# Hymba step, last stage: the gather of a chunk's second-choice rows is issued one chunk behind the first-choice gather instead of three

## What is computed

```python
def _layer(...):
    mix, ... = _mixer(x, ...)
    x = _layer_norm(DEEPNORM_ALPHA * x + mix, ln1_g, ln1_b)
    x = _layer_norm(DEEPNORM_ALPHA * x + _hmoe(x, ...), ln2_g, ln2_b)

def _hmoe(x, ...):
    # two experts per token: wts (n, 2), eid (n, 2)
    gate = jnp.einsum('nk,nke->ne', wts, jax.nn.one_hot(eid, N_EXPERTS))
    a = jnp.einsum('nd,edf->nef', xt, w1)
    u = jnp.einsum('nd,edf->nef', xt, w3)
    hdn = jax.nn.silu(a) * u * gate[..., None]
    return jnp.einsum('nef,efd->nd', hdn, w2)
```

## Time and profile before

| | us |
|---|---|
| median of 3 executions | 1198.36 |
| lowest, highest | 1190.17, 1199.01 |
| the profiled execution | 1197.36 |
| its span in the trace | 1195.4 |

### The profile page before, as it was taken

One profiled execution on the slowest core, in us unless ns is written; L12 is line 12 of the kernel. 1 busy time (PEld: TensorE's weight loads), 2 busy tenths in 40 slices (PEclk: granted clock), 3 DMA queues, 4 the chain that ended last, 5 costly groups with the idle time before them and its releaser, 6 DMA issues.

```text
span 1195.4 us, 17214 instructions
## 1 busy us (share of the span) xinstructions
PE 1009.2 (84%) x6738; PEld 606.5 (51%) x6738; DVE 600.9 (50%) x1007; ACT 248.9 (21%) x532; POOL 244.1 (20%) x208
## 2 busy tenths in 40 slices
PE   7999999979999695999999999842788999799500
PEld 4666666645656354566666666442344455345200
DVE  1550133347777767787787778353122333231046
ACT  1542111121211122132223222110111111011023
POOL 0000000001110132353454344000000000450175
PEclk9999999989999898999999999955799999899755
DMA  9010101020000244000100110507799787948496
GB/s 385 35 70 1 71 1 71 0 74 1 1 1 1 80 163 178 4 33 19 36 36 1 36 36 18 194 27 289 317 327 351 283 322 299 381 177 305 141 219 181
DMA packets 30680, 154.28 MB, mean 129 GB/s; under 512 B 5546, under 2 KB 5994, under 8 KB 21274
## 3 DMA queue, kind: packets, MB, share of 16 engines
q1 hardware_dynamic: 24938, 130.17, 28.9%
q0 software_dynamic: 5248, 18.94, 6.0%
q10 hardware_dynamic: 432, 4.35, 1.0%
HBM read 321.52 MB, written 23.82 MB: 289 GB/s over the span
## 4 chain that ended last, share of the span: by engine, by line
PE 78%; DMA 9%; DVE 7%; issue 3%; POOL 1%; ACT 1%; SPq 1%; DVEq 0%; ACTq 0%; POOLq 0%
PE psum L1657 17%; PE psum L772 9%; PE psum L1708 9%; PE psum L759 9%; PE psum L1334 5%; PE psum L1311 5%; PE psum L1345 5%; PE psum L800 4%; DMA weight_slots<-in_w_gate 3%; DMA x_cm<-y_slots,hg_k 2%; DMA hg_decay<-in_w_up 2%; PE psum L734 1%; PE psum L1675 1%; PE psum L1296 1%; POOL x_cm L1425 1%
## 5 line engine op out<-in xcount | busy, mean ns | idle before, releaser
L1657 PE MATMUL psum<-x_cm,weight_slots 128*128 128x344 f32 x720 | 209.0, 453 | 0.0
L1657 PEld LDWEIGHTS psum<-x_cm,weight_slots 128*128 128x128 f32 x720 | 136.7, 190 | 71.7 <-issue 1.1
L1708 PE MATMUL psum<-weight_slots,x_cm 128*128 128x512 f32 x256 | 113.6, 597 | 0.0
L1334 PE MATMUL psum<-weight_slots,scratch 128*32 128x256 f32 x1280 | 78.6, 401 | 22.8 <-DMA weight_slots<-in_w_gate 12.8
L1311 PE MATMUL psum<-conv_qk,scratch 128*32 128x512 f32 x320 | 77.2, 627 | 9.3 <-issue 7.1
L1311 PE MATMUL psum<-hg_q,scratch 128*32 128x512 f32 x160 | 77.0, 627 | 0.0
L1311 PE MATMUL psum<-hg_k,scratch 128*32 128x512 f32 x160 | 77.0, 627 | 0.0
L1411 POOL DMA_INDIRECT scratch<-x_rows,hg_k x20 | 19.3, 966 | 282.4 <-PE psum L1296 197.4
L1345 PE MATMUL psum<-conv_qk,scratch 128*32 128x256 f32 x640 | 74.3, 386 | 3.1 <-DMA hg_decay<-in_w_up 2.9
L1708 PEld LDWEIGHTS psum<-weight_slots,x_cm 128*128 128x128 f32 x256 | 48.0, 193 | 54.1 <-issue 54.1
L1345 PE MATMUL psum<-hg_decay,scratch 128*32 128x256 f32 x640 | 74.3, 386 | 0.0
(11 more groups left out here) (355 smaller groups left out, 1648.0 us busy)
## 6 DMA issues: line engine op xcount, KB each, us to landing
weight_slots<-in_w_gate SPq DMA_DIRECT2D x80, 1024.0 KB
conv_qk<-in_w_up SPq DMA_DIRECT2D x40, 1024.0 KB
hg_decay<-in_w_up SPq DMA_DIRECT2D x40, 1024.0 KB
conv_qk<-in_w_down SPq DMA_DIRECT2D x40, 1024.0 KB
hg_k<-in_w_down SPq DMA_DIRECT2D x20, 1024.0 KB
hg_q<-in_w_down SPq DMA_DIRECT2D x20, 1024.0 KB
weight_slots<-in_w_in SPq DMA_DIRECT2D x6, 2048.0 KB, 7.6
y_slots<-scratch SPq DMA_DIRECT2D x20, 512.0 KB, 6.4
```

Source lines behind the costliest of these rows:

```text
L1334: m = mm(PS[lane, 2, 0:FF], xgT[i][:, k, lane], w_gate[q][:, k], start=(k == 0), stop=(k == KD - 1))
L1657: i = mm(PS[0:m, idx % 4, 0:PIECE], lhs_of(k), xT[:, k, n * PIECE:(n + 1) * PIECE], start=(k == 0), stop=(k == KD - 1))
L1708: i = mm(PS[:, bank, :], xT[:, k, c * P:(c + 1) * P], w_slot(g)[:, k, :], start=(k == 0), stop=(k == KD - 1))
```

## The change

In the loop that issues the gathers, the second gather of chunk c - 3 followed the first of chunk c; now it is the second gather of chunk c - 1. All instructions, their number, their sizes and every other engine's program stay as they are.

```diff
-        for c in range(NTT + 3):
+        for c in range(NTT + 1):
             if c < NTT:
                 if c >= 6:
                     pool.wait_ge(y_sems[c % 6], 32)
                 add_rows(0, c)
-            if c >= 3:
-                pool.wait_ge(y_sems[(c - 3) % 6], 32 * ((c - 3) // 6) + 16)
-                add_rows(1, c - 3)
+            if c >= 1:
+                pool.wait_ge(y_sems[(c - 1) % 6], 32 * ((c - 1) // 6) + 16)
+                add_rows(1, c - 1)
```

## The result

The changed kernel takes 1202.02 us (median of 20 runs, 1197.95 to 1211.73) against 1197.75 us for the kernel before (20 runs, 1190.17 to 1203.25). The ratio is 1.0044, with a 95% interval of 1.0023 to 1.0065; the forecast was 1203.3 us, a ratio of 1 + 4.9 / 1198.36 = 1.0041.

A forecast was written before the change was run, and what follows sets the result against it. The prediction took full DMA engines as the bound in the last 70 us, DVE at the end. A 1.1 us hole plus POOL's late start made +4.9 us on 1198.36 us: 1203.3 us, range 1195 to 1209 us.

The forecast's parts named there:

- The first wait: Ahead of second 0, POOL stands idle 2.5 us for first 0's landing and issues at 1135.4 us.
- The waits in the middle: After second 0, three gathers at most are out, yet the DMA engines stay full; cost nothing, up to 4.8 us uncovered.
- the sum: All terms of the change together: +4.9 us, of which 1.1 us is the hole and the rest POOL's late start.
- the 0.9 us: Slack per middle chunk: second c could land 6.6 us after first c, the queue lets it land after 7.5 us.
- the hole: DMA engines idle around second 0, which lands at 1141.7 instead of 1140.6 us: 1.1 us for everything behind.
- the step that decides: Second 8 waits for first 8, directly behind second 6; POOL's bias additions begin about 1178.3 us instead of 1171.11 us.
- The line of POOL and DVE: At the end, six POOL additions and DVE's L1607 for chunks 6, 7, 8 exclude each other: 17.9 us, ending 1196.9 us.
- The early chunks: Second 0 lands 4 us and second 4 some 3.9 us earlier; worth nothing, as DVE's end hangs on chunks 6 to 8.
- A: Rival, 8%: a short queue serves gathers faster, 2.1 us each, second 6 landing at 1166.9 us; -4.2 us, 1194.2 us.
- B: Rival, 9%: at the end POOL's additions and DVE's L1607 run side by side; +0.9 us, 1199.3 us.
- C: Rival, 15%: the queue runs dry in each of six chunks, 0.8 us each; 4.8 us on top, 1208.1 us.
- D: Rival, 8%: the change does not show, gathers hide it and the tail is DVE's; 1198.4 us.

The follow-up runs named there:

- after_again: The changed kernel run once more on one chip with between_again, nothing altered: stage 69.7 us, ratio 1.0052 to the kernel before.
- between_again: lag1_between run once more, on the same chip as after_again: stage 67.2 us, ratio 1.0036 to the kernel before.
- lag1_between: The changed kernel with POOL's bias additions of chunks 3 and 4 done between its last gathers: stage 66.0 us, ratio 1.0044 to the kernel before.
- head3_tail1: Order of the kernel before up to second 1, then the changed kernel's from first 5 on: stage 67.1 us, ratio 1.0018 to the kernel before.
- all-DVE pair: The changed kernel and the kernel before, each with all nine bias additions on DVE: stages 64.6 and 63.2 us, ratios 1.0018 and 0.9990.

## Why the prediction was right, and where it was off

In us from the first gather's issue, so that the traces can be compared:

| step | forecast | trace after |
|---|---|---|
| second 0 issued | 6.6 | 6.7 |
| second 0 landed | 12.9 | 13.0 |
| second 6 landed | 47.2 | 49.1 |
| second 7 issued, landed | 44.8, 51.1 | 46.9, 53.6 |
| second 8 issued | 48.1 | 49.6 |
| POOL's first addition | 49.5 | 50.5 |
| last addition ends | 68.1 | 69.9 |

- *The first wait* was right to 0.1 us in where it ends: the wait is there, and a gather that finds the engines idle lands 6.3 us after its issue. Its length was given as 2.5 us of idle time, where the prediction's own times (1132.6 to 1135.4 us) make 2.8 us and the trace has 3.17 us, which holds the 0.30 us between two issues. The landings of first 0 and second 0 in the trace after, two such gathers:

```profile
DMA to landing us min/median/max: 6.4/6.4/6.4
...
DMA to landing us min/median/max: 6.3/6.3/6.3
```

- *The waits in the middle* are where the sum was mis-sized. The prediction cost them at nothing "with the 0.9 us as its cover", 4.8 us without it. Second 6 landed 3.0 us later than before, and only 1.1 us of it is the hole; 1.9 us are left. Nearly all of it was lost once, right behind the hole: seconds 0 and 1 landed 6.8 us apart (13.0 and 19.8 us), where two gathers at 2.5 us make 5.0. In other traces with this head it was less or nearly as much: 6.5 us in after_again, 6.1 us in between_again, 5.4 us in lag1_between. So the cover of 0.9 us held for the stretched issues, which took 1.70 to 1.79 us, not 2.38 us, and for which 0.1 us is left. The engines were not idle meanwhile: their share was 1.03 to 1.07 from 1138 to 1148 us, at 197 to 201 GB/s in place of 207 to 215 in the trace before, and 5% less explains 0.3 to 0.4 us. Where the rest went stays open.
- *Second 8, "the step that decides"*, puts the weight on the smaller of two waits. POOL's late start is there, 8.2 us of it (50.5 against 42.3 us, forecast 7.2), but POOL waits 3.40 us for first 7 and then only 0.89 us for first 8. Of the 0.89 us, 0.30 us is what stands between any two issues; an earlier first 8 would by this estimate have gained POOL 0.6 us. No run moved first 8 alone; that the tail order as a whole costs 3.9 us is shown by head3_tail1.
- *The line of POOL and DVE* is right in mechanism and size. It began at 1177.13 us and ended at 1196.48 us, 19.35 us; six additions at 2.34 us and four L1607 at 1.08 us make 18.4 us. Of the 1.0 us left, 0.4 us is the overlap of the first addition's record with the issue before it (below), the rest handovers. The forecast had chunk 5's L1607 ahead of the line; it came into it, since second 6 was later and POOL was first. Its length of 5.72 us is two of POOL's additions and itself. That the 3.9 us come from POOL's additions is shown by head3_tail1, which has them with chunk 6 on time, and by the all-DVE pair, which does not have them. One sign of being right was not met: the last two additions were to have "no or little wait for DVE", and the last four each waited 1.22 to 1.24 us, as before. This is no idle time of the line: DVE's L1607 ran in it, itself held up by the addition before.
- *The early chunks are worth nothing by themselves*: right, and their lead was shorter than forecast. Chunk 0 was 3.9 us early, chunk 4 only 1.7 us where 3.9 was forecast, chunk 5 0.8 us late where it was to be early, and chunk 6 2.8 us late.
- *The sum* was 4.9 us; the stage says 6.7 us, the ratio 1.0044 says 5.3 us (2.8 to 7.8). Split at chunk 6's statistics the forecast was 0.7 + 4.2 us (47.2 us into the stage, then 20.9 us), and the trace has 2.8 + 3.9 us. So the term of the tail was right, and the one before it came out at nearly four times its size. That the median of 1202.0 us stands so near the 1203.3 us is in part luck: the kernel before settled at 1197.75 us, not at the 1198.36 us from which the forecast started, and the ratio is on the low side of the stage.
- *The rivals.* A (served faster) and B (side by side) are out: no gather was served faster, and the two engines did not overlap. C (the queue runs dry in every chunk) did not happen: from 1138 to 1174 us the share was 1.02 to 1.15 in every window of 2 us but one of 0.91. Of its two signs only the spacing was seen, once (6.8 us between chunks 0 and 1). What was lost, 1.9 of C's 4.8 us, was lost at one place. D is out with the late additions.

## What to carry to other kernels

Where gathers are issued in pairs with a wait between, a smaller distance brings early results to those who wait first, but the end of a stage is set by its last chunks and by what is queued behind the last wait on the issuing engine: here six additions. Before shortening such a distance, ask what the in-order engine still has to do after its last wait, and whether that work excludes another engine's. And if a short last piece costs as much as a full one, don't put it last.

## What the runs showed of the hardware that was not expected

- DVE waiting for POOL's two-input operation did not get the next turn: two additions of 2.34 us went ahead of its L1607 (5.72 us in the trace after, 5.90 us in after_again, 5.73 us in head3_tail1). In later rounds, where POOL had to wait for DVE, they alternated (1.78 us).
- The first addition behind a gather's issue is recorded too long and too early. In lag1_between and between_again such additions took 2.78 to 2.94 us instead of 2.34 us, and they appear before the issue ahead of them is over (second 7 of between_again: 1178.49 + 1.59 = 1180.08 us, the addition from 1179.53 us, 0.55 us of overlap and 0.60 us too long). In the trace after the overlap is 0.43 us and two additions take 5.10 us, 0.42 us more than 2 x 2.34. So starts on POOL are rough by about half a us, and whether POOL or DVE asked first at 1177.6 us can't be read.
- A store of a finished chunk, issued by SP at 1154.95 us in the trace before with five gathers out, seems to move only from about 1159.5 us on; the rate rises from 209 to 211 GB/s to 283 at 1160 us. In the trace after the store of 1150.73 us had three gathers ahead of it, its queue's first packet moved between 1152 and 1153 us, and the rate rose at 1154 us (293 GB/s). So the longer queue goes with the longer delay. This was read off two traces, not tested.
